# Another order of work for ScalarE and VectorE in the expert loop of a diffusion step

## The reference: what must be computed

```
hid = silu(t @ w1[e]) * (t @ w3[e])     # w1, w3: 1024 x 256 for each expert
hid = hid * gate                        # the two gates of a token
out += hid @ w2[e]                      # w2: 256 x 1024
```

## Time and profile before

| | us |
|---|---|
| median of three runs | 701.74 |
| lowest and highest run | 699.96, 710.32 |
| the profiled execution | 708.24 |
| its span, first to last instruction | 706.5 |
| expert loop in it, about | 445 to 670 |
| TensorE, VectorE, ScalarE, POOL busy over the span | 595.2, 432.0, 308.7, 189.8 |
| mean granted TensorE clock over the span | 0.931 |

### The profile page before, as it was taken

How to read it: one execution, slowest core, us unless ns; L and a number is a source line. 1 busy time by engine, 2 the same in 40 slices (tenths; PEclk the granted TensorE clock), 3 DMA queues, 4 the chain that set the end, 5 groups by cost and what they waited for, 6 DMA issues and landing times.

```text
span 706.5 us, 8796 instructions
## 1 busy us (share of the span) xinstructions
PE 595.2 (84%) x3024; PEld 466.1 (66%) x3024; DVE 432.0 (61%) x663; ACT 308.7 (44%) x500; POOL 189.8 (27%) x211
## 2 busy tenths in 40 slices
PE   3879996999998999999999974798979697989800
PEld 3438885998993576677787852676767586777600
DVE  3329456776029555455544578587777777787538
ACT  5215141313112455346501432477676768777421
POOL 2040222110003000000400012446757364652423
PEclk9978998999999999999999975999999999999955
DMA  9980200332624075041543161589889988888264
GB/s 334 387 269 1 103 17 21 113 127 69 238 74 169 1 284 193 1 172 71 198 192 147 60 215 48 216 332 365 291 324 345 328 303 313 315 311 311 79 263 188
DMA packets 42033, 137.56 MB, mean 195 GB/s; under 512 B 6444, under 2 KB 6460, under 8 KB 34192
## 3 DMA queue, kind: packets, MB, share of 16 engines
q1 hardware_dynamic: 32032, 115.91, 45.1%
q0 software_dynamic: 8976, 20.68, 8.1%
q10 hardware_dynamic: 992, 0.55, 0.3%
HBM read 131.83 MB, written 16.29 MB: 210 GB/s over the span
## 4 chain that ended last, share of the span: by engine, by line
PE 48%; DMA 20%; DVE 19%; ACT 5%; issue 4%; POOL 1%; SPq 1%; ACTq 0%; DVEq 0%; POOLq 0%
DMA big<-w 15%; PE bank L1316 10%; PE bank L1318 10%; PE bank L1317 10%; DVE big_r L1109 6%; PE bank L1487 3%; DMA big<-w_ada 3%; ACT big_r L760 3%; PE bank L1449 2%; PE bank L1465 2%; PE bank L1432 2%; PE bank L1312 2%; DVE hu L1050 2%; PE bank L1537 1%; PE bank L1451 1%
## 5 line engine op out<-in xcount | busy, mean ns | idle before, releaser
L1316 PE MATMUL bank<-big_r 128*128 128x512 f32 (+1 forms) x264 | 101.2, 383 | 3.3 <-DVE hu_r L920 3.3
L1109 DVE TENSOR_TENSOR big_r<-big,big_r 128x2048 fp32r<-128x2048 f32 x40 | 91.4, 2288 | 19.9 <-ACT big_r L760 19.7
L760 ACT ACTIVATE big_r<-big 128x2048 fp32r<-128x2048 f32 x40 | 76.7, 1917 | 48.9 <-DMA big<-w 47.5
L1317 PE MATMUL bank<-big_r 128*128 128x512 f32 x200 | 79.7, 399 | 0.0
L1318 PE MATMUL bank<-big_r 128*128 128x512 f32 (+1 forms) x184 | 66.9, 363 | 0.0
L1318 PE MATMUL bank<-big_r,hu_r 128*128 128x512 f32 x160 | 64.1, 401 | 0.0
L1316 PEld LDWEIGHTS bank<-big_r 128*128 128x128 f32 x264 | 54.8, 208 | 9.9 <-issue 3.4
L1316 PE MATMUL bank<-hu_r,rs_r 128*128 128x512 f32 x80 | 35.3, 442 | 27.3 <-ACT rs L809 16.3
L1317 PEld LDWEIGHTS bank<-big_r 128*128 128x128 f32 x200 | 42.8, 214 | 6.5
L588 POOL COPY small<-small 128x1 uint32 (+1 forms) x20 | 27.8, 1391 | 70.9 <-ACT rs L809 40.2
L515 POOL TENSOR_TENSOR small<-small 128x8 f32<-128x8 f32 (+1 forms) x15 | 21.5, 1432 | 92.2 <-DVE small L946 57.8
(11 more groups left out here) (257 smaller groups left out, 1402.2 us busy)
## 6 DMA issues: line engine op xcount, KB each, us to landing
big<-w SPq DMA_DIRECT2D x40, 1024.0 KB
big<-w_ada SPq DMA_DIRECT2D x12, 2048.0 KB, 14.7
big<-w_in SPq DMA_DIRECT2D x5, 2048.0 KB, 9.6
cc<-w SPq DMA_DIRECT2D x10, 1024.0 KB
xt<-w SPq DMA_DIRECT2D x10, 1024.0 KB
big<-slot_out SPq DMA_DIRECT2D x10, 512.0 KB, 7.3
big<-w_out SPq DMA_DIRECT2D x2, 2048.0 KB, 10.7
hu<-ada_rows POOLq DMA_DIRECT2D x6, 512.0 KB, 11.9
```

The source lines that it names most:

```text
L760: nc.scalar.activation(w13_hi[p][:, v, :], w13_raw[v], ACT.Copy).then_inc(w13_hi_ready, 1)
L1109: V.tensor_tensor(w13_lo[p][:, v, :], w13_raw[v], w13_hi[p][:, v, :].bitcast(F32), ALU.subtract).then_inc(w13_lo_ready, 1)
L1316: T.matmul(out, lhs[0], rhs[0], start=start, stop=False)
L1317: T.matmul(out, lhs[0], rhs[1], start=False, stop=False)
```

## The change

Both functions keep all their calls; the calls change places. On ScalarE the two weight halves of block b+2 go behind the tokens, the hidden rows and the store, with `silu` between them. On VectorE the tokens' rest goes first, then w2's rest and the hidden rows' rest, then half 0, `hidden`, and half 1.

```diff
--- before.py
+++ after.py
@@ -810,13 +810,13 @@
                                          ACT.Copy).then_inc(y_act, 1)
 
             def act_block(b, p, nth):
-                w13_rounded(b + 2, 0, p)
                 hgT_rounded(b + 2, p)
-                w13_rounded(b + 2, 1, p)
                 hidT_rounded(b)
                 if not (isinstance(b, int) and b == 0):
                     store(b - 1, 1 - p, nth - 2)
+                w13_rounded(b + 2, 0, p)
                 silu(b + 1)
+                w13_rounded(b + 2, 1, p)
                 w2_rounded(b + 1, 1 - p, nth)
 
             act.nop().then_inc(y_act, 2 + 2 * BEHIND)
@@ -1263,12 +1263,12 @@
                 V.tensor_tensor(hid[p], banks[6][:, DE:2 * DE], sil, ALU.mult).then_inc(hid_ready, 1)
 
             def dve_block(b, p):
+                hgT_rest(b + 2, p)
                 w2_rest(b, p)
+                hidT_rest(b)
                 w13_rest(b + 2, 0, p)
-                hgT_rest(b + 2, p)
-                hidT_rest(b)
+                hidden(b + 1, 1 - p)
                 w13_rest(b + 2, 1, p)
-                hidden(b + 1, 1 - p)
 
             for v in range(2):
                 w13_rest(1, v, 1)
```

## The result

| | before | after |
|---|---|---|
| median of the runs, us | 705.64 (4 runs) | 721.06 (4 runs) |
| ratio after to before | | 1.0222, 95% interval 1.0162 to 1.0282 |
| profiled execution, us | 708.24 | 720.58 |
| up(1) starts at | 454.61 | 456.43 |
| from up(1) to up(19) | 203.07 | 211.21 |

The change makes the kernel 2% slower.

What follows compares the result with a forecast made beforehand. No engine was full; the loop waited on round trips of weight loads, ScalarE and VectorE. Terms 1.2 + 0 + 10.5 = 11.7 us took the profiled 708.24 to 719.9, by ratio 713.3 us from median 701.74; range 702 to 727.

Steps and rivals of the forecast that it cites:

- the gap before `down`: TensorE's idle time until the rounded hidden rows are ready; claimed to go away, up to 27.3 us.
- the ring of 11.39 us: Waits from up(b+1) through TensorE, ScalarE and VectorE to up(b+2); claimed 11.39 us a block, +1.2 us over the loop.
- The loads, taken at nothing: Weight-half loads in the loop, 7.0 us left for each; claimed to cost 0, at most 7.5 us.
- the fifteen pieces of before: Load pieces in the old kernel's chain of waits, mean 7.06 us; nine said to exceed 7.0, by 7.5 us together.
- The clock, 7 blocks at 1.5 us: TensorE's clock falling to half after the new gap before up; claimed in 7 of 17 blocks, +10.5 us.
- Behind up(19) both orders are the same: After the last loop block, claimed that old and changed kernels run the same order; no cost counted there.
- What would show it: Profile signs, such as gaps before up put down to VectorE's weight rest and a granted clock under 0.96 in the loop.
- low clock everywhere: Rival: half clock in nearly every loop block, 1.2 + 25.5 us, 734.9 profiled or 728 us, ratio 1.038; chance 0.17.
- no low clock: Rival: no half clock after the gaps in the loop, only 1.2 us, ratio 1.002, 703 us; chance 0.24.
- loads as late as now: Rival: loop loads stay late, +19.2 us on top of the forecast, ratio 1.027, 721 us; chance 0.12.
- The faster case: Rival: TensorE bounds the loop at 9.36 us a block, a gain of up to 34.6 us, 667 us; chance 0.03.

Runs made afterwards that it cites:

- store_late: The changed kernel with ScalarE's store of block b-1 moved behind the second weight half: 710.53 us, ratio 1.0014 to the kernel before.
- store_early: The changed kernel with ScalarE's store of block b-1 moved right behind the tokens, ahead of the hidden rows: 709.00 us, ratio 1.0018 to the kernel before.
- more_traffic: The changed kernel with an extra, unread 0.5 MB DRAM-to-DRAM copy per block behind w2's load: 721.2 us in one run.
- filled: The changed kernel with four spare matmuls of 256 columns between token_T(b+2) and up(b+1): 714.69 us, ratio 1.0120 to the kernel before.
- before_filled: The kernel before with three spare matmuls of 256 columns ahead of down(b): 708.46 us, ratio 1.0029 to the kernel before.

## Why the prediction was right

**The forecast** was 713.3 us, and 719.9 against the profiled execution's own 708.24; that execution of the changed kernel took 720.58. The range of 702 to 727 held the median. The median came out higher than 713.3 in part because the median of before, shown as 701.74, is 706.1 to 706.4 over the runs of this study. Measured, the ratio is 1.022 and not 1.0165. I had given 0.58 to a time within 2% and 0.39 to slower, and it lies just beyond 2%. So the mechanism came true, and the size of the whole was forecast somewhat low.

**Removed, the gap before `down`:** right. It is 0.0 in the loop; 25.2 us went, as 2.06 of the 27.3 lay behind up(19) and stayed.

**Added, the ring of 11.39 us:** right to 0.04 us (11.43 on average, 10.64 for the first block where I had 10.67), and its cost against the profiled execution of before, forecast as 1.2 us, was 1.9. store_late and store_early show by a removed step that it is the ring, and more_traffic that the loads are hardly on it. The weak point of this term is what it is compared with, one execution's 203.07: filled, at the full clock, is 8.3 us slower than before by the medians, so against a typical execution of before this term may be several us too small. No trace settles that.

**The loads, taken at nothing:** right. ScalarE waited 0.5 us for them, and they landed after 5.0 us in the median. Of the fifteen pieces of before eight exceed 7.0 us, not nine; together they do so by 7.5 us, as I had it. The Trainium skill (DMA: Bandwidth & Descriptors, Anatomy of one DMA) gives its fit of 2.0 us plus bytes over 436 GB/s for DMAs issued through GpSimd. The prediction left that out, and these loads are issued by SyncE; as an estimate from that fit the 4.4 us for 1 MiB came within 0.6 us of the measured median.

**The clock, 7 blocks at 1.5 us:** the mechanism is right (filled), the size of one is right (1.57 us), the number was four and not seven, in two executions. So this term was 6.3 us and not 10.5. The other 4.2 us of the total came from outside the loop. The sum of 11.7 us against 12.3 was closer than its parts, and that is luck.

**Behind up(19) both orders are the same:** true for the orders, yet this execution took 2.3 to 2.4 us more there. Ahead of the last `down` both kernels have a gap of 2.06 us. In both executions of the changed kernel the clock fell behind it, in that of the kernel before it did not. The executions of this study with no half-clock stretch in the two blocks behind up(19) took 48.8 to 49.4 us from there to the last instruction, those with one such stretch 50.5 to 51.2. I had put no low clock there.

**What would show it:** I wrote that the gap before `up` would be put down to VectorE's rest, and that the chain would run through ScalarE and VectorE. Both were wrong as readings of a profile, since it writes "issue" for 17 of these 18 gaps. I also expected a granted clock under 0.96 in the loop; it was 0.97. Four low stretches in a longer loop are no larger a share than before, and the clock's mean says nothing about whether they lie on the path.

**The rivals:** low clock everywhere would have been 735 in the profiled execution, no low clock 709; loads as late as now did not come. That rival's 721 us is the measured median to the microsecond, so the time alone would not have told it from the forecast; its mechanism is absent, since ScalarE waited 0.5 us for loads. The faster case had no support in any run.

## What to carry to other kernels

Before work is moved behind a wait on an in-order engine, follow the wait round: if what it releases leads back to the same engine in the next iteration, the steps add up to a period that no overlap can hide, and here it could be summed from starts in the old trace to a few hundredths of a microsecond. A gap that disappears at one place is worth only the difference between the old period and the new one, and where it reappears decides whether a lower clock behind it is paid for. Change the orders of two engines that feed each other together, and move work that isn't needed in the ring into the time in which an engine waits for it, as store_early does. And profile the kernel before more than once if its time spreads: the ring's length was exact here, and what it was compared with was not.

## What the runs showed of the hardware that I had not expected

- Gaps of the same length, 1.8 to 1.9 us, brought TensorE's low clock in four blocks of 17 and not in the others, and in another execution again in four of 17, two of them the same. 1.9 us of spare matmuls in the gap kept it at 1.00 throughout.
- POOL's busy time in the loop fell from 118.8 us to 69.0 over the same stretch. In store_late it was 93.0. I did not look into why.
- Kernels whose loop is a ring spread less: the changed kernel over 4.6 us in six runs and filled over 5.4 in ten, the kernel before over 22.3 in 31, 11.2 in 23 and 12.4 in 23. But before_filled, paced by loads, spread over only 8.5 in ten, so that the ring makes the difference is not shown.
